# Sixteen experts without a loop on TensorE, and attention pair by pair

## The reference, cut to what matters

```python
h = rms_norm(x, norm1_g) * (1 + scale1) + shift1
z = h @ w_in                                        # q, k, v of 8 heads x 64, and 2 x 512 convolution columns
attn_out = neighbourhood_attention(q, k, v, rpb)    # grid 64 wide; window of 8 rows x 16 columns for each query
conv_out = conformer_conv(ca, cg, ...)
x = x + gate1 * (concatenate([attn_out, conv_out]) @ w_out)
h2 = rms_norm(x, norm2_g) * (1 + scale2) + shift2
aff = softmax(h2 @ w_router)                        # 16 experts; each takes its top 64 (prompt) and 128 (sample) tokens
hid = silu(xe @ w_gate[e]) * (xe @ w_up[e])         # 1024 -> 2816, for each expert e
y[idx] += (hid @ w_down[e]) * g                     # 2816 -> 1024
x = x + gate2 * y
```

## Time and profile before

| | us |
|---|---|
| median of 3 runs | 3620.57 |
| lowest, highest | 3617.51, 3620.6 |
| the profiled execution | 3617.59 |
| its span | 3615.8 |
| busy in the span: PE, DVE, ACT | 3318.3, 2357.2, 1926.2 |
| attention, first score to last copy | 630.4 to 831 |
| experts' products on TensorE | 1124 to 3598 |

### The profile page before, as it was taken

The page is one execution under the profiler, slowest core; times in us unless marked ns, Lnnn a source line. Parts: engine busy times, 40 slices in busy tenths (PEclk is TensorE's granted clock), DMA queues, the critical chain, the costliest instruction groups (busy, mean ns, idle before and its releaser), DMA issues.

```text
span 3615.8 us, 50525 instructions
## 1 busy us (share of the span) xinstructions
PE 3318.3 (92%) x18494; PEld 2888.6 (80%) x18494; DVE 2357.2 (65%) x3652; ACT 1926.2 (53%) x3186; POOL 142.0 (4%) x208
## 2 busy tenths in 40 slices
PE   8498877898926999999999999999999999999998
PEld 1386655456825999999999999999999999999997
DVE  0367882574365677676777767676676767767675
ACT  0623332464524666666566666665656666666664
POOL 0000000000001000000001001000000000000000
PEclk9699988799967999999999999999999999999999
DMA  8401113604234476665757666475665757666572
GB/s 316 135 27 50 50 38 99 210 36 166 109 134 157 178 294 218 247 233 210 262 205 263 220 230 252 184 288 218 240 241 190 279 202 263 232 227 250 187 276 91
DMA packets 143696, 696.58 MB, mean 193 GB/s; under 512 B 12420, under 2 KB 39556, under 8 KB 119940
## 3 DMA queue, kind: packets, MB, share of 16 engines
q1 hardware_dynamic: 132196, 659.75, 49.1%
q0 software_dynamic: 7168, 25.17, 3.1%
q10 hardware_dynamic: 4132, 8.65, 0.8%
HBM read 655.73 MB, written 37.80 MB: 192 GB/s over the span
## 4 chain that ended last, share of the span: by engine, by line
PE 68%; DVE 2%; issue 1%; DMA 0%; POOL 0%; ACT 0%; POOLq 0%; DVEq 0%
PE psG L1200 31%; PE psG L1202 14%; PE psY L1216 5%; PE psY L1219 5%; PE psY L1217 5%; PE psY L1218 4%; PE psY L1220 4%; DVE idxu L1392 1%; DVE affT L1394 1%; DVE vals L1390 1%; PE psG L1167 0%; PE psG L1168 0%; DMA xg_s<-xhat_d,inow 0%; ACT xst L1301 0%; DVE xe L1413 0%
## 5 line engine op out<-in xcount | busy, mean ns | idle before, releaser
L1200 PE MATMUL psG<-xe,w_gu_hi_part 128*128 128x384 f32 x5632 | 1638.3, 361 | 24.9 <-issue 20.7
L1202 PE MATMUL psG<-xe,w_gu_lo_part 128*128 128x192 f32 x5632 | 1414.1, 251 | 0.0
L1200 PEld LDWEIGHTS psG<-xe,w_gu_hi_part 128*128 128x128 f32 x5632 | 1062.8, 189 | 38.2 <-issue 26.2
L1202 PEld LDWEIGHTS psG<-xe,w_gu_lo_part 128*128 128x128 f32 x5632 | 1080.5, 192 | 7.4
L1403 DVE TENSOR_TENSOR w_gu_lo_part<-raw_gu,w_gu_hi_part 128x1024 fp32r<-128x1024 f32 x704 | 859.1, 1222 | 117.9 <-ACT w_gu_hi_part L1312 117.8
L1312 ACT ACTIVATE w_gu_hi_part<-raw_gu 128x1024 fp32r<-128x1024 f32 x704 | 741.3, 1055 | 12.9 <-DMA raw_gu<-in_w_gu 12.9
L1437 DVE TENSOR_TENSOR gu<-psG,low 128x384 f32<-128x384 f32 x352 | 196.0, 557 | 599.8 <-ACT low L1342 599.8
L1408 DVE TENSOR_TENSOR w_dn_lo_part<-raw_dn,w_dn_hi_part 128x1024 fp32r<-128x1024 f32 x352 | 431.3, 1225 | 0.8 <-ACT w_dn_hi_part L1323 0.8
L1342 ACT ACTIVATE low<-psG 128x384 f32<-128x384 f32 x352 | 172.2, 489 | 446.8 <-PE psG L1202 446.8
L1323 ACT ACTIVATE w_dn_hi_part<-raw_dn 128x1024 fp32r<-128x1024 f32 x352 | 367.8, 1045 | 0.8 <-PE psY L1220 0.8
L1301 ACT ACTIVATE xst<-psG,modv,a 128x128 f32<-128x128 f32 (+1 forms) x256 | 96.1, 428 | 393.1 <-PE psG L1202 326.2
(11 more groups left out here) (157 smaller groups left out, 3453.3 us busy)
## 6 DMA issues: line engine op xcount, KB each, us to landing
raw_gu<-in_w_gu SPq DMA_DIRECT2D x176, 2048.0 KB, 7.8
raw_dn<-in_w_down SPq DMA_DIRECT2D x176, 1024.0 KB, 8.8
aw<-in_ada_w SPq DMA_DIRECT2D x12, 2048.0 KB, 9.0
bias<-in_bias SPq DMA_DIRECT2D x8, 1536.0 KB, 11.0
w_raw<-in_w_in SPq DMA_DIRECT2D x20, 512.0 KB, 5.3
qk_d<-zg SPq DMA_DIRECT2D x8, 768.0 KB, 3.7
qk<-qk_d SPq DMA_DIRECT2D x8, 768.0 KB, 11.2
out<-wo_raw SPq DMA_DIRECT2D x12, 512.0 KB, 2.6
```

What stands on the lines that cost most here:

```text
L1200: pe.matmul(bank[:, 0:2 * CAP], wh, xe[:, k, :, :].rearrange("p a b -> p (a b)"), start=(k == 0), stop=False, skip_group_check=True)
L1202: mm = pe.matmul(bank[:, 0:CAP], wl, xe[:, k, 0, :], start=False, stop=(k == KD - 1), skip_group_check=True)
```

## The change

In `attend` TensorE's order is rewritten by pairs: both scores of pair u, then `pv(u-2)`, then both turns of pair u-1. The scores get four banks instead of three and `psO` two instead of three. In `experts` TensorE's sixteen experts are written out one after the other with constants for e; ACT, DVE, POOL and SP keep their loops.

```diff
-        psS = ps(c, "psSc", [P, 3, 512])
+        psS = ps(c, "psSc", [P, 4, 512])
         psT = ps(c, "psPT", [P, 2, 512])
-        psO = ps(c, "psOh", [P, 3, 512])
+        psO = ps(c, "psOh", [P, 2, 512])
...
-                    if i >= 3:
-                        pe.wait_ge(s_biased, i - 2)
+                    if i >= 4:
+                        pe.wait_ge(s_biased, i - 3)
...
-                    if u >= 3:
-                        pe.wait_ge(o_out, u - 2)
+                    if u >= 2:
+                        pe.wait_ge(o_out, u - 1)
...
-                for i in range(UNITS + 4):
-                    if i < UNITS:
-                        scores(i)
-                    if 3 <= i < UNITS + 3:
-                        turn(i - 3)
-                    if i >= 5 and i % 2:
-                        pv((i - 5) // 2)
+                for u in range(PAIRS + 2):
+                    if u < PAIRS:
+                        scores(2 * u)
+                        scores(2 * u + 1)
+                    if u >= 2:
+                        pv(u - 2)
+                    if 1 <= u < PAIRS + 1:
+                        turn(2 * u - 2)
+                        turn(2 * u - 1)
...
-                expert(0, True, False)
-                with pe.Fori(1, EXPERTS - 1) as e:
-                    expert(e, False, False)
-                expert(EXPERTS - 1, False, True)
+                for e in range(EXPERTS):
+                    expert(e, e == 0, e == EXPERTS - 1)
```

More of the change, by code:

```diff
@@ L736, in scores @@
                         "p (r c) -> p r c", c=GRID_W)[:, :, KEY_COL0[j]:KEY_COL0[j] + K_COLS]
-                    pe.matmul(psS[:, i % 3, 0:rows * K_COLS], q, k, start=True, stop=True).then_inc(s_done, 1)
+                    pe.matmul(psS[:, i % 4, 0:rows * K_COLS], q, k, start=True, stop=True).then_inc(s_done, 1)
                 def turn(i):
@@ L754, in pv @@
                             pe.wait_ge(v_loaded[first + m], 16 * 4 * COL_BLOCKS)
-                    if u >= 3:
-                        pe.wait_ge(o_out, u - 2)
+                    if u >= 2:
+                        pe.wait_ge(o_out, u - 1)
                     for m in range(rows // 4):
-                        mm = pe.matmul(psO[:, u % 3, 0:2 * P], v[:, (first + m) * COL_BLOCKS + j, h * DH:(h + 2) * DH],
+                        mm = pe.matmul(psO[:, u % 2, 0:2 * P], v[:, (first + m) * COL_BLOCKS + j, h * DH:(h + 2) * DH],
                                        pT[:, u % 2, m, :, :].rearrange("p w q -> p (w q)"),
@@ L782, in _ @@
                             dve.wait_ge(p_ready, i - 1)
-                        dve.tensor_tensor_reduce(out=sc[:, i % 2, 0:w], in0=psS[:, i % 3, 0:w],
+                        dve.tensor_tensor_reduce(out=sc[:, i % 2, 0:w], in0=psS[:, i % 4, 0:w],
                                                  in1=bias[:, h % 4, PATTERN[j], at:at + w], scale=1.0, scalar=-3e38,
@@ L806, in _ @@
                                 "p (r c) -> p r c", c=GRID_W)[:, :, j * Q_COLS:(j + 1) * Q_COLS]
-                            m = dve.tensor_copy(out, psO[rows, u % 3, w * P:(w + 1) * P].rearrange("p (r c) -> p r c", c=Q_COLS))
+                            m = dve.tensor_copy(out, psO[rows, u % 2, w * P:(w + 1) * P].rearrange("p (r c) -> p r c", c=Q_COLS))
                         m.then_inc(o_out, 1)
```

## The result

The changed kernel takes 3563.48 us (median of four runs, 3562.49 to 3566.02), the kernel before 3619.04 us beside it (3614.93 to 3620.6). The ratio is 0.9842, with a 95% interval of 0.9828 to 0.9857: 1.6% faster. Predicted were 3571 us, in a range of 3556 to 3590. The profiled execution took 3562.92 us, with a span of 3561.1 us, 54.7 us shorter than before. In every run of this document the mean granted clock was 0.950 to 0.957 but in one of the four of `short_jumps`, which took 3705.99 us at 0.824 and is left out of that run's median. Lines of `attend` on VectorE and ScalarE have moved by two, and so have those of `experts` on TensorE: L1202 and L1204 are the old L1200 and L1202, L1218 to L1222 the old L1216 to L1220, L832 the old L830.

The account below looks back on a forecast made before the run. The prediction took TensorE to bound both experts and attention. From 3617.6 us it took 22.8 for jumps, 6.4 for clock falls and 18 for attention, giving 3570.4, stated as 3571 us, range 3556 to 3590.

Parts of the forecast that it names:

- The jumps: Experts on TensorE: writing out the loop removes thirteen jumps back of 1.79 us each, 22.8 us in all.
- The falls of the clock: Experts on TensorE: with the pauses, four falls to 1.2 GHz go, 1.59 us each, 6.4 us in all.
- Attention: Attention stage: the pairwise order on TensorE saves 18 us, with ends of 0 and 33 us.
- The chain through ScalarE: Attention: the product with v waits for ScalarE's copy; 3.49 us per 384-key pair, TensorE stalling about 0.5 us.
- first six pairs: Start of attention: first pairs stay at 1.2 GHz; the second score saves some 1.6 us in each of three, 3 us more.
- The scores do run side by side: Attention rival: the two scores of a pair run alone, gain 5.5 us instead of 18, 3583 us; chance 0.15.
- DVE was not the bound: Attention rival: DVE becomes the bound, gain 33 instead of 18 us, 3556 us; chance 0.15.
- Pauses inside the written-out experts: Experts rival: fetching new instructions brings pauses inside the experts, all 29 us of the loop stay, 3600 us; chance 0.04.
- that rival: Attention rival: the clock falls, 75 us more than before if held through the stage, 3663 us; chance 0.06.
- TensorE as the only bound: Attention, by a skill page: TensorE alone sets 3.00 us a pair, saving about 33 us; not used in the sum.
- Spread: Whole kernel: without the jumps, less spread between runs was expected; runs of the kernel before differ by 3 us.

Follow-up runs that it names:

- short_jumps: The changed kernel with a two-round loop, holding only a wait long met, behind each of experts 1 to 13; 3564.45 us, median of three runs.
- hint_jump: The changed kernel with TensorE's experts 1 to 14 a loop again, its jump back announced at the top of each round; 3563.87 us.
- pv_between: The changed kernel with the product with v between the two turns of a pair on TensorE instead of ahead of both; 3555.4 us.
- act_order: The changed kernel, but for the second unit of a pair ScalarE copies out the transposes before it takes the exponential; 3546.26 us.
- scores_apart: The changed kernel, but the second score of each pair waits until the first is done; 3584.4 us.
- loop_only: The kernel before with only TensorE's experts written out, attention as before; 3584.45 us.
- attn_only: The changed kernel with TensorE's loop over experts 1 to 14 put back, the pairwise attention kept; 3592.72 us.
- two_per_round: The changed kernel with TensorE's experts 1 to 14 as a loop of seven rounds of two experts; 3577.43 us.

## Why the prediction was right

The direction, the mechanisms and the order of size held, and the median lies 7.5 us under the forecast of 3571 us. Term by term, in the profiled executions:

**The jumps.** 22.8 us were predicted. The start distances at the thirteen boundaries add up to 25.8 us before and 3.0 us after, which is 22.8 us. The cause, the far jump back and the fetch of its target, is shown by three runs and by the instruction packets: announced or short jumps cost nothing that shows, and six far ones cost 11.4 us of listed wait.

**The falls of the clock.** 6.4 us were predicted for four. None is left in the changed kernel's experts between the first few microseconds and the end, nor in those of the other nine kernels without pauses. The kernels with pauses have eight falls behind 32 pauses (4 of 13, 3 of 13, 1 of 6). In these thirteen executions no fall came in the experts without a pause in front of it; which pause brings one they don't show.

**What I left out in the experts.** 31.7 us were saved where 29.2 were predicted. An expert without a fall took 154.81 us before, less a pause of 2.34 us between starts, plus 0.23: 152.70 us. Now it takes 152.59 us. TensorE lost 0.11 us more in getting going, thirteen times, 1.4 us. And expert 0 took 155.43 us before and 154.73 after, since the low clock with which the stage begins ended sooner after its start in this execution, which is 0.7 us and luck. With these two the terms give 31.3 of the 31.7 us. The 1.6 us of the mix stage, which I did not predict, come with one fall of the clock of 3.4 us less in it (one after, two before); but in `hint_jump` and `pv_between`, with none, the stage takes 292.7 and 291.6 us, so the falls don't explain it, its cause is open, and that it came out shorter is luck.

**Attention.** 18 us were predicted, 21.1 measured. The chain through ScalarE was right as it stood: 3.49 us for a pair of 384 keys against 3.45, with a stall of 0.38 against "about 0.5". The product with v at 1.3 us behind the scores' start, ScalarE's copy as what it waits for, DVE waiting for the scores in the end: each step is in the rows. `act_order` shows it from the other side, since moving that copy alone takes the stall away. From the seventh pair, at 672.86 us before and 665.45 us after, to the stage's end 13.9 us were saved. These are 30 pairs of 384 keys and 12 of 256, and the same terms give 30 x 0.45 + 12 x 0.07 = 14.3 us. The mis-sized term is that of the first six pairs. The 18 us left them 3.7 us, and they saved 7.2 us. Of these 6.2 us lie in the fifth and sixth, which took 12.40 us before, all but the end of it at the lower clock, and take 6.22 us now that the clock comes back at 658.5 instead of 672.8 us. In `scores_apart`, where it comes back at 655.0 us and the scores do not run side by side, the first six pairs save as much, 7.3 us, so it is the clock and not the pairing. That I had not foreseen: I took the speed of the first pairs as given and counted only work. That the surplus went the right way is luck.

**The rivals.** The scores do run side by side although each has a wait in front, and without that the gain would be what `scores_apart` leaves. DVE was not the bound; it stood at 85% in the steady part, and became it, together with TensorE, only in `act_order`. Pauses inside the written-out experts did not appear. The clock did not fall in attention at 86% busy and with six transposes in a row, so the 75 us of that rival did not come. The rule of the Trainium skill, "TensorE: Matmul & The Clock Gate", section PE-mode transpose, that such work does not hold the clock up, did no harm here; whether it holds by itself no run here shows, as scores and products always stand between.

**Drains.** TensorE as the only bound would have given 3.00 us a pair. The changed kernel measures 3.45, so that gives too much; with the stall removed, in `act_order`, the pair takes the 3.00 us. The Trainium skill, "TensorEngine Tiling (Array Packing)", section Key Properties, states that different tiles can load weights and multiply in parallel. The trace agrees for the two scores of a pair, 0.92 us for both against 0.91 us for one. What a drain costs by itself no run here shows.

**Spread.** Predicted to shrink, which is not shown. The changed kernel's four runs lie within 3.5 us and the four of the kernel before beside them within 5.7 us; but of the other kernels without pauses four runs lie within up to 7.8 us (`loop_only`), and of `attn_only` and `two_per_round`, with pauses, within 5.2 and 4.5 us.

What stays open: why the clock comes back sooner under the new order. In both profiles with the old order of attention it stays low until 672.8 and 682.5 us; in the eleven with a pairwise order, until 654.6 to 667.3 us. Scores side by side are not needed for it, as `scores_apart` has it too. Nothing was tried that separates the order from what it does to TensorE's busy share.

## What to carry to other kernels

A pause of the bounding engine that the profile puts down to "issue", once in each round of a long loop, was the jump back here; compare it with a boundary that is passed without a jump, and before writing the loop out try to announce the jump, which was worth as much here and kept the program short. Products over 64 rows in different halves of the partitions are worth issuing next to each other. When an in-order engine's list is changed, follow the ring through the other in-order engines once around: it told the new pair time to 0.04 us, and it pointed at the copy on ScalarE whose swap gave 17 us more.

## What the runs showed of the hardware

- A jump back over a few instructions costs nothing that can be measured on TensorE, one over an expert 1.75 us on the mean in the kernel before (1.3 to 2.2 us beyond the usual 0.23), one over two experts 2.06 us. In `attn_only` the jump over one expert cost 1.90 us (1.4 to 2.4 us).
- Announcing the jump did not only hide the fetch but nearly ended it: 51 packets of instructions in the whole execution instead of 168, and 148 when written out, and none during thirteen rounds of the loop. I expected the same number of fetches, only earlier.
- After a pause of under 2.5 us TensorE's clock fell to 1.2 GHz in 8 of 32 cases, for about 3.4 us each time, and cost 1.6 us. Without a pause it never fell in the experts, at 16 experts in each of ten kernels.
- In attention TensorE kept the full clock at 86% busy.
